# A conditioned decoder block on eight cores: weight casts moved later, modulation products placed further back, last output columns in token halves

## The reference

```python
mod = silu(c) @ w_mod + b_mod            # 9 vectors of 1024: shift, scale, gate x 3
x = x + 0.5 * gt1 * swiglu_ffn(ada_rmsnorm(x, g1, sh1, sc1), w_ffn1_in, w_ffn1_out)
h = ada_rmsnorm(x, g_mix, sh2, sc2)
u_val, u_gate, u_x, u_y = split(h @ w_in)             # 4 x 512
y_conv = silu(layernorm(conv31(u_val * sigmoid(u_gate))))
y_rnn  = gelu(u_y) * rglru(conv4(u_x))                # gated linear recurrence
x = x + gt2 * (concat(y_conv, y_rnn) @ w_out)
x = x + 0.5 * gt3 * swiglu_ffn(ada_rmsnorm(x, g3, sh3, sc3), w_ffn2_in, w_ffn2_out)
y = ada_rmsnorm(x, g_final, f_shift, f_scale)         # f_* from silu(c) @ w_fmod + b_fmod
```

## Time and profile before

| | us |
|---|---|
| three runs | 2369.35, 2373.75, 2509.9; median 2373.75 |
| profiled execution: its own time | 2375.25 |
| its span on the slowest core (core 7) | 2373.7 |
| spans of the eight cores | 2348.4 to 2373.7 |
| PE busy | 2249.8 (95%) |
| DVE busy | 1324.7 (56%) |
| ACT busy | 956.6 (40%) |
| POOL busy | 287.0 (12%) |

### The profile page before, as it was taken

One profiled execution on the slowest core, in us unless ns is written; L12 is line 12 of the kernel. 1 busy time (PEld: TensorE's weight loads), 2 busy tenths in 40 slices (PEclk: granted clock), 3 DMA queues, 4 the chain that ended last, 5 costly groups with the idle time before them and its releaser, 6 DMA issues.

```text
span 2373.7 us, 34088 instructions; the slowest of 8 cores (2348.4 to 2373.7 us)
## 1 busy us (share of the span) xinstructions
PE 2249.8 (95%) x10864; PEld 1006.1 (42%) x10864; DVE 1324.7 (56%) x2131; ACT 956.6 (40%) x1473; POOL 287.0 (12%) x552
## 2 busy tenths in 40 slices
PE   1999998998999899899999999999999999999995
PEld 0444443443444344344444444444444444444442
DVE  5323225524433485674776476487487588477522
ACT  3313213303110533553565536436536556454512
POOL 0011110020000110201110120111111111120000
PEclk9999999999999999999999999999999999999998
DMA  9899798899866685654665665556456566564452
GB/s 258 189 232 215 194 206 214 214 212 243 214 187 164 191 223 170 190 167 141 194 207 158 207 200 191 154 171 227 153 178 214 160 171 222 158 186 138 151 177 89
DMA packets 122704, 446.86 MB, mean 188 GB/s; under 512 B 18864, under 2 KB 19248, under 8 KB 121520
## 3 DMA queue, kind: packets, MB, share of 16 engines
q1 hardware_dynamic: 90864, 330.44, 44.7%
q0 software_dynamic: 31664, 114.23, 21.5%
HBM read 426.87 MB, written 71.30 MB: 210 GB/s over the span
## 4 chain that ended last, share of the span: by engine, by line
PE 85%; DMA 8%; issue 2%; DVE 2%; ACT 2%; POOL 1%; SPq 0%; DVEq 0%; ACTq 0%; POOLq 0%
PE ps L457 83%; DMA sb_x<-x 2%; PE ps L1097 2%; DMA sb_cs<-wmod 2%; DMA sb_fs<-b 1%; DMA sb_fs<-w 1%; DMA sb_hidB<-wmod 1%; DMA sb_cs<-bm 1%; DVE sb_rstdm L441 1%; DMA x<-sb_x 0%; SPq L417 0%; POOL sb_urep L1087 0%; ACT sb_hb L434 0%; POOL sb_x L417 0%; ACT sb_ntmp L434 0%
## 5 line engine op out<-in xcount | busy, mean ns | idle before, releaser
L457 PE MATMUL ps<-sb_hb,sb_fs 128*128 128x512 bf16 x5632 | 1245.6, 382 | 35.5 <-DMA sb_fs<-w 14.2
L457 PEld LDWEIGHTS ps<-sb_hb,sb_fs 128*128 128x128 bf16 x5632 | 553.9, 98 | 711.8 <-issue 62.5
L457 PE MATMUL ps<-sb_hidA,sb_fs 128*128 128x512 bf16 x2288 | 505.7, 379 | 0.8 <-DVE sb_hidA L441 0.8
L434 ACT ACTIVATE sb_sgf<-ps 128x512 f32<-128x512 f32 x352 | 206.5, 593 | 406.8 <-PE ps L457 364.3
L457 PEld LDWEIGHTS ps<-sb_hidA,sb_fs 128*128 128x128 bf16 x2288 | 223.9, 98 | 269.6 <-issue 1.3
L441 DVE TENSOR_TENSOR sb_hidA<-ps,sb_sgf 128x512 bf16<-128x512 f32 x286 | 195.4, 688 | 227.1 <-PE ps L457 161.4
L457 PE MATMUL ps<-sb_hb,sb_cs 128*128 128x512 bf16 x992 | 224.2, 379 | 4.5 <-DMA sb_cs<-bm 3.4
L1087 POOL DMA_DIRECT2D sb_urep<-sb_ub x256 | 131.0, 520 | 694.5 <-PE ps L457 435.6
L437 DVE SCALAR_TENSOR_TENSOR sb_x<-ps,sb_gth,sb_x 128x512 f32<-128x512 f32 x128 | 96.0, 750 | 174.8 <-PE ps L457 174.4
L434 ACT ACT_TABLE_LOAD x102 | 130.9, 1283 | 154.4 <-PE ps L457 134.1
L437 DVE SCALAR_TENSOR_TENSOR sb_ux<-sb_ub,sb_vecs,sb_ux 128x512 f32<-128x512 bf16 x240 | 179.7, 749 | 10.0 <-DVE sb_ux L437 0.9
(11 more groups left out here) (104 smaller groups left out, 1338.6 us busy)
## 6 DMA issues: line engine op xcount, KB each, us to landing
sb_fs<-b SPq DMA_DIRECT2D x396, 512.0 KB, 4.4
sb_cs<-bm SPq DMA_DIRECT2D x78, 512.0 KB, 4.1
sb_x<-x POOLq DMA_DIRECT2D x96, 256.0 KB, 7.9
sb_cs<-wmod SPq DMA_DIRECT2D x46, 512.0 KB, 12.6
sb_rs<-bm SPq DMA_DIRECT2D x34, 512.0 KB, 5.0
sb_fs<-w POOLq DMA_DIRECT2D x33, 512.0 KB, 9.9
b<-sb_fs SPq DMA_DIRECT2D x33, 512.0 KB, 8.8
b<-w POOLq DMA_DIRECT2D x33, 512.0 KB, 10.3
```

The costliest lines, as they stand in the source:

```text
L434: return Op(ACT, lambda h: [h.activation(out=out, in_=in_, func=func, **kw)], reads, writes, cost, tset)
L457: out.append(h.matmul(ps[:, bank, :], lhsT=l, rhs=r, start=(first and k == 0), stop=(last and k == n - 1)))
```

## The change

1. Only slabs 0 to 27 of the second FFN (`W2A = 28`) are cast from memory to memory. Slabs 28 to 32, the last five of the output blocks, are loaded with a cast by POOL into the ring at the first FFN2 job (tile 0), and written back by SP for the later jobs. `w_in` goes from 24 to 16; the other 12 casts spread over 0.85 of the next 33 ticks.
2. A modulation product is placed once the model's PE clock is 20 us (before: 8) past its slab's landing.
3. In the last FFN2 job (tile 7) output groups 5, 6 and 7 are computed by token halves: the three groups for tokens 0 to 255, then for 256 to 511, each with its own stream for the norm (`o_half`). A small Exp brings the activation table in ahead. The stores go by SP, two column groups of 256 tokens each.
4. The eight stores of a tile share one semaphore (`s_y[t % 4]`), and all eight column groups of the slot wait for its final value.
5. The convolution's code is rewritten with `CVD = (0,)` and `CVP = (1, 2, 3)`; with these values it emits the same operations in the same order.

```diff
+W2A = 28
...
 def write_back(k):
     si = k % NFS
-    core.emit(dma(SP, b1_d[k], fslots[si]..., [r_fs[si]], [r_b1[k]], s_fw[si], MB // 2))
+    dst, r_dst = wbdst.pop(k)
+    core.emit(dma(SP, dst, fslots[si]..., [r_fs[si]], [r_dst], s_fw[si], MB // 2))
...
+    if g == 0:
+        wbdst[s] = (b1_d[s], r_b1[s])
-    if half == 2:
+    if half == 2 and (half, jobs[g][1]) == (2, [0]) and s >= W2A:
+        wbdst[len(fplan)] = (b2_d[s], r_b2[s])
+        fplan.append(load_cast(w2_d[s]))
+    elif half == 2:
         fplan.append(load_bf(fslots, r_fs, s_fs, b2_d[s], r_b2[s]))
...
-casts2 = [(w2_d[s], b2_d[s], r_b2[s]) for s in range(NF1)]
+casts2 = [(w2_d[s], b2_d[s], r_b2[s]) for s in range(W2A)]
...
-    yield lambda: PE.clock > r_ms[k % NM].tw + 8.0 or fring.freed >= 3 * NF1 - 2
+    yield lambda: PE.clock > r_ms[k % NM].tw + 20.0 or fring.freed >= 3 * NF1 - 2
...
-    w_in = 24
+    w_in = 16
...
-    bg.extend([(npair + (j + 0.5) / (NF1 - w_in) * NF1 * 0.6, "w") for j in range(NF1 - w_in)])
+    bg.extend([(npair + (j + 0.5) / (W2A - w_in) * NF1 * 0.85, "w") for j in range(W2A - w_in)])
...
+def out_halves(si, kb, freed, gth, r_gth):
+    yield flag("o5")
...
+    for hf in range(2):
+        cols = slice(HT * hf, HT * hf + HT)
+        for oc in range(OCF, 8):
...
+                    prs.append((sl[:, idx % 16, :], hids[0][:, k, cols]))
...
+                yield mmh(b, prs, rr + r_hid[0][lo:hi_], lo == 0, hi_ == 22)
+            yield stt(xs[si][:, oc, cols], ps[:, b, 0:HT], gth[:, oc:oc + 1], xs[si][:, oc, cols], ...)
...
+def o_half(hf):
...
+    for oc in range(OCF, 8):
+        if oc == 7:
+            yield mmh(bank, [(ones_bf[:], accb[:, 0:HT])], [r_accb, r_ones], True, False)
+            yield act(sgm[:, hf:hf + 1], hstate[:, 0:1], AF.Exp, [r_hst[0]], [r_sgm], tset="E", cost=0.2)
...
+    yield mmh(bank, [(ones_bf[:], last_b[:, 0:HT])], [r_last, r_ones], False, True)
+    yield [act(acc, ps[:, bank, 0:HT], AF.Ln, ...), act(acc, acc, AF.Exp, ...)]
+    for fc in range(8):
+        yield stt(xt[:, fc, cols], xt[:, fc, cols], gsf[:, fc:fc + 1], acc, ...)
+        yield act(xt[:, fc, cols], xt[:, fc, cols], AF.Identity, ...)
+        if fc % 2 == 1:
+            yield dma(SP, y_d[t, fc - 1:fc + 1, :, cols]..., xt[:, fc - 1:fc + 1, cols], ..., s_yl, MB // 4)
...
-    yield dma(PL, y_d[t, fc], xt[:, fc, :], [r_xt[fc]], [], s_y[fc], MB // 4)
+    sy = s_y[t % 4]
+    yield dma(PL, y_d[t, fc], xt[:, fc, :], [r_xt[fc]], [], sy, MB // 4)
+for fc in range(8):
+    r_xt[fc].r[sy] = sy.val
```

More of the change, by code:

```diff
@@ L369, in build_program @@
         s_x1 = [newsem(f"s_xs{k}") for k in range(4)]
-        s_y = [newsem(f"s_y{k}") for k in range(8)]
+        s_y = [newsem(f"s_y{k}") for k in range(4)]
+        s_yl = newsem("s_yl")
         s_fs = [newsem(f"s_fs{k}") for k in range(NFS)]
@@ L829, in ffn_in, with halves, mmh, fn @@
             flags.add(("fin", j))
+        HT = T // 2
+        OCF = 5
+        r_xh = []
+        r_oh = []
+        def halves(res):
+            out = []
+            for hf in range(2):
+                for r0 in res:
+                    r = Res()
+                    r.w = r0.w
+                    r.tw = r0.tw
+                    r.tr = r0.tr
+                    r.r = dict(r0.r)
+                    out.append(r)
+            n = len(res)
+            return [out[:n], out[n:]]
+        def mmh(bank, prs, reads, first, last):
+            n = len(prs)
+            def fn(h):
+                out = []
+                for k, (l, r) in enumerate(prs):
+                    out.append(h.matmul(ps[:, bank, 0:HT], lhsT=l, rhs=r, start=(first and k == 0), stop=(last and k == n - 1)))
+                return out
+            return Op(PE, fn, reads, [r_bank[bank]], 0.11 * n)
@@ new lines, in out_halves @@
+        def out_halves(si, kb, freed, gth, r_gth):
+            yield flag("o5")
+            r_xh.extend(halves(r_x[si]))
+            r_oh.extend(halves([r_ro]))
+            for hf in range(2):
+                streams.append(Stream(f"O{hf}", o_half(hf), b_m))
+            for hf in range(2):
+                cols = slice(HT * hf, HT * hf + HT)
+                for oc in range(OCF, 8):
+                    got = yield lambda: bankF.take(1)
+                    b = got[0]
+                    for lo, hi_ in ((0, 14), (14, 22)):
+                        prs = []
+                        rr = []
+                        for k in range(lo, hi_):
+                            idx = oc * 22 + k
+                            sk = kb + idx // 16
+                            yield fring.has(sk)
+                            sl, r_sl = fring.at(sk)
+                            prs.append((sl[:, idx % 16, :], hids[0][:, k, cols]))
+                            if r_sl not in rr:
+                                rr.append(r_sl)
+                        yield mmh(b, prs, rr + r_hid[0][lo:hi_], lo == 0, hi_ == 22)
+                    yield stt(xs[si][:, oc, cols], ps[:, b, 0:HT], gth[:, oc:oc + 1], xs[si][:, oc, cols], ALU.mult, ALU.add,
+                              [r_bank[b], r_gth], [r_xh[hf][oc]], 0.45)
+                    bankF.give(b)
+                    flags.add(("x3h", oc, hf))
+            while freed < kb + NF1 - FC:
+                fring.done(freed)
+                freed += 1
@@ L888, in oevict @@
                         r_x1[g[j]].tw = op.end
-            for oc in range(8):
+            tail = xflag == "x3c" and g[0] == n_tiles - 1
+            for oc in range(OCF if tail else 8):
                 for j, t in enumerate(g):
@@ L921, in ffn @@
             yield from oevict(oev)
+            if tail:
+                yield from out_halves(x_of(g[0]), kb, freed, gth, r_gth)
         def tick(op, phase1):
@@ L1127, in c_gen @@
                 bankM.give(bv)
-                if c == 0:
-                    streams.append(Stream(f"V{i}", v_gen(i), dict(b_m, dve=0)))
-                if c == 1:
+                if c in CVD:
+                    streams.append(Stream(f"V{i}.{c}", v_gen(i, c), b_v))
+                if c == 1 and CVP[0] < 2:
                     yield spread(0)
             flags.add(("glu", i))
-            for c in range(1, 4):
+            for c in CVP:
+                if c == 2 and CVP[0] == 2:
+                    yield cring.has(k0 + 4)
+                    cring.done(k0 + 4)
+                    yield spread(1)
                 k = k0 + 4 + c // 2
@@ L1273, in o_gen @@
                 st = stat_o()
+                if t == n_tiles - 1:
+                    for fc in range(OCF):
+                        yield flag(("x3c", t, fc))
+                        yield from accum(st, xt[:, fc, :], r_xt[fc])
+                    flags.add("o5")
+                    return
                 yield from stats(xt, r_xt, st, before=lambda fc, t=t: flag(("x3c", t, fc)))
@@ L1367, in prep_inputs @@
             shared[:, V_RCW + 4 * cc + k] = rcw[k, cc * 128:(cc + 1) * 128]
-    shared[:, V_CW:V_CW + NCONV] = f(inputs["conv_w"][0])[:, 0:128].T
+    for j, cc in enumerate(CVD):
+        shared[:, V_CW + NCONV * j:V_CW + NCONV * (j + 1)] = f(inputs["conv_w"][0])[:, 128 * cc:128 * cc + 128].T
     def blocks(w, rows, cols):
```

87 lines of the change are left out of this document (60 added, 27 removed).

## The result

The changed kernel takes 2389.82 us (median of 6 runs) against 2376.53 for the kernel before (6 runs). The ratio is 1.006, 95% interval 1.0045 to 1.0075: slower by some 14 us. I had forecast 2361.5 us, 12 faster.

The account below looks back on a forecast made before the run. PE bounds the kernel, busy 2249.8 of 2373.7 us. Pauses -11, later casts 0, ring slabs +1, semaphore +3 and tail -4.9 sum to -11.9: 2363.35 us profiled, 2361.5 for the runs; range 2347 to 2378.

Parts of the forecast that it names:

- One semaphore for a tile's stores: Five reloads of x slots: all eight loads wait for the last store, 0 to 3.3 us each; 3 us slower taken.
- the reloads have no slack: Rival, at POOL's wait before reloads: five each 3.3 us late at PE, a casting slab late too; 2386 us, chance 0.15.
- The pauses among the pairs: 330 to 600 us: three PE pauses cost 21.6 us; later products and fewer casts save half, 11 us.
- Five slabs cast into the ring: Tile 0's output stage: casting loads land just within their lead by the median; 1 us slower taken.
- The casts that come later: After the pairs: 12 casts, same load for eight ticks longer; 0 us, with 2 us either way.
- The tail: Last output groups to the end: token halves and SP stores save 4.9 us, between -6.5 and +1.6.
- the weight loads: Rival, half-width matmuls of the tail: 98 ns loads not covered by 108 ns matmuls; +6.5 us, 2368 us, chance 0.08.

Follow-up runs that it names:

- e1: The changed kernel with each column group's store given its own semaphore again; ratio 0.9997 (0.9973 to 1.0022) against the kernel before.
- e2: The kernel before with only the shared semaphore for a tile's eight stores added; ratio 1.0072 (1.0056 to 1.0088) against the kernel before.
- e5: The kernel before with only the casts edited (W2A = 28, w_in = 16, factor 0.85, five slabs cast into the ring); ratio 1.0017 (0.9997 to 1.0037).
- e6: The kernel before with only the tail by token halves and its stores by SP; ratio 0.9983 (0.9968 to 0.9998), 4 us.

## Why the prediction was wrong

**One semaphore for a tile's stores: the step that failed.** It said that the planner knows of the wait and puts other matmuls ahead, that a reload costs between 0 and 3.3 us, and it took 3 us for all five. The change adds only a token to be waited for; the time at which the model frees a column group stays that of its own store. e1 and the changed kernel have the same order of matmuls, as have e2 and the kernel before. Measured, the edit costs 15 to 17 us, where 3 were taken. That this meets the step's upper bound of 16.5 is chance: not five reloads cost 3.3 us each, but two show as pauses of 4.4 and 4.5 us at the matmul with ones, one more at an eviction, and some 6 us are the lower clock behind the pauses. The reload looked at came 4.7 us later, not 3.3, and of this 2.3 us lie between the end of the last issue and the first use (10.6 us for 8.3). The rival "the reloads have no slack" named place and mechanism and gave 2386 us, with a chance of 0.15; its other part, a casting slab late by 5 us, did not happen, and its sum had left those 5 us out.

**The pauses among the pairs: the step that failed second.** I took half of 21.6 us, 11. The measured gain is none: 15.3 us idle before, 16.1 after. Three intermediate quantities came as forecast or better (DMA share 0.78 for 0.81, ring slabs 5.5 us for 9.5, DVE's waits for w_mod from 68.2 us to 1.2), but the one on which the pauses hung did not: loads of x took 14.5 us, where 11 were forecast, and 25.46 at the boundary. What was late next was the x tile, as the text itself had said; and the planner moved the matmul with ones forward, which the text had not thought of. The forecast summed two edits on one stall and halved the sum, where the right question was which arrival ends the wait once both are gone. (A slip without weight: 2363.35 less 1.5 is 2361.85, not 2361.5.)

**Five slabs cast into the ring: right.** Forecast 1 us. In the changed kernel, core 0, the five slabs' time to landing from 1060 to 1140 us:

```profile
DMA to landing us min/median/max: 6.2/8.0/9.2
```

All lie under the leads of 10.0 to 13.5 us, and PE waited for none.

**The casts that come later: right within the noise** (0 forecast, 2 us either way). Idle time from 769 to 1010 us, where the later casts lie, is 16.1 us after and in e5 for 14.4 before, with 8.4 to 19.4 between the cores; e5 as a whole gave 0.9997 to 1.0037.

**The tail: right.** Forecast -4.9 us; e6 gives -4, and from the last norm's matmul with ones to the end the changed kernel takes 148.4 us (2240.01 to 2388.4) against 153.7 (2220.01 to 2373.7), 5.3 less. Two of its terms were off and cancel: PE's part of this stretch, up to its last output matmul, grew by 1.6 us (forecast 0.8), and from ACT's end to the end of the span it takes 11.2 us for 12.7, 1.5 less (forecast 0.4). The half matmuls came at 0.109 us, so 132 of them take 0.1 us more than 66 whole ones at 0.216; the weight loads did not show. The Trainium skill's section "Back-to-back issue gap" ("TensorE: Matmul & The Clock Gate") led to an estimate of 0.098 us by interpolation between its sustained values. Its formula for a single matmul gives 109 ns, and with that the trace agrees.

## What to carry to other kernels

A semaphore shared by several stores turns "this piece is free" into "all pieces are free"; price it by the time from the last store to the first use of the refilled buffer, and look at whether the planner's own clock knows of it. In a kernel whose order is fixed beforehand, a faster transfer can be given away by a planner that then places the consumer earlier: correct the planner's landing times first, then take load off the queues. Where several arrivals can end one wait, edits tested one at a time can all measure as nothing: so it was here with the products, the casts and x planned late, which together with the later planned reloads and the tail's 0.2% gave 1.2%. And look at the DMA share of the few microseconds in which the awaited load runs, not at the mean of the stretch.

## What the runs showed of the hardware

Eight loads of 256 KB issued in one burst behind a landed store were first used 10.6 us after the end of the last issue (1657.00 to 1667.56), against 8.3 us (1647.92 to 1656.26) where seven of them had gone out earlier. In both cases ACT's first use waits for all eight. At the pair boundary the last load of such a burst needed 25.46 us; the DMA share in those 25 us was 1.03, though the mean from 330 to 600 us was 0.78. I had expected landings to shorten with the mean load of the stretch; ring slabs did (14.2 to 5.5 us), bursts of x hardly did (16.8 to 14.5 us). That the burst and the transfers issued just before it fill the DMA engines by themselves fits the share, but no run spread the burst, so it is not shown.

Half-width matmuls (128x256, each with its own weight load of 98 ns) started 109 ns apart, full ones 216 ns apart.
